# Levels 1 to 3 of a batched triangular inverse on all four quarters of the array, in a two-layer trunk kernel

## What is computed

```python
def chunk_gated_delta_rule(q, k, v, g, beta):
    C = GDN_CHUNK                     # 64
...
    a_mat = jnp.where(strict, jnp.einsum('bhnik,bhnjk->bhnij', k_beta, k) * decay, 0.0) + jnp.eye(C, dtype=f32)
    tri = functools.partial(lax.linalg.triangular_solve, left_side=True, lower=True, unit_diagonal=True)
    u = tri(a_mat, v * beta[..., None])
    w = tri(a_mat, k_beta * jnp.exp(g)[..., None])
...
    S0 = jnp.zeros((B, H, N, v.shape[-1]), f32)
    _, o = lax.scan(step, S0, xs)
```

## Time and profile before

| | |
|---|---|
| time, median of 3 runs | 1431.37 us (1431.27 to 1431.80) |
| the profiled execution's own time | 1431.33 us |
| its span, first to last instruction | 1429.6 us |
| PE busy | 1396.9 us (98%) |
| DVE busy | 668.8 us (47%) |
| ACT busy | 599.9 us (42%) |
| the four tiles' levels 1 to 3 | 11.63, 11.84, 11.85 and 13.17 us |

### The profile page before, as it was taken

How to read it: one execution, slowest core, us unless ns; L and a number is a source line. 1 busy time by engine, 2 the same in 40 slices (tenths; PEclk the granted TensorE clock), 3 DMA queues, 4 the chain that set the end, 5 groups by cost and what they waited for, 6 DMA issues and landing times.

```text
span 1429.6 us, 24988 instructions
## 1 busy us (share of the span) xinstructions
PE 1396.9 (98%) x10495; PEld 1147.7 (80%) x10495; DVE 668.8 (47%) x1112; ACT 599.9 (42%) x866; POOL 526.5 (37%) x239
## 2 busy tenths in 40 slices
PE   7999999999999999999999999999999999999998
PEld 5787778889878888888889977775688888888887
DVE  4665767788753314122144358936543223131231
ACT  5524763445545313232234465568635223131331
POOL 3544332111133543444345224332333443444341
PEclk9999999999999999999999999999999999999999
DMA  5332300000133233223224122210033223323221
GB/s 151 89 101 77 83 20 3 4 4 3 62 104 103 89 96 103 96 88 112 94 89 119 30 89 89 88 60 1 1 102 105 88 88 108 99 88 111 95 89 59
DMA packets 128977, 110.13 MB, mean 77 GB/s; under 512 B 10742, under 2 KB 126576, under 8 KB 128880
## 3 DMA queue, kind: packets, MB, share of 16 engines
q1 hardware_dynamic: 128000, 107.12, 24.1%
q10 hardware_dynamic: 880, 1.59, 0.3%
HBM read 106.60 MB, written 2.10 MB: 76 GB/s over the span
## 4 chain that ended last, share of the span: by engine, by line
PE 91%; DVE 3%; ACT 2%; POOL 2%; issue 1%; DMA 1%; SPq 0%; ACTq 0%; DVEq 0%; POOLq 0%
PE ps L570 23%; PE ps L571 23%; PE ps L575 23%; PE ps L707 5%; PE ps L1141 2%; PE ps L1151 1%; PE ps L1162 1%; PE ps L715 1%; PE ps L607 1%; PE ps L1116 1%; POOL pw_lo L2382 1%; PE ps L938 1%; PE ps L939 1%; PE ps L945 1%; PE ps L722 1%
## 5 line engine op out<-in xcount | busy, mean ns | idle before, releaser
L2469 POOL TENSOR_TENSOR w_lo<-lower,w_hi 128x2048 fp32r<-128x2048 f32 x83 | 385.6, 4645 | 523.6 <-ACT w_hi L1233 508.8
L570 PE MATMUL ps<-h_hi,w_hi 128*128 128x512 f32 x736 | 288.5, 392 | 1.2 <-ACT h_hi L1546 0.8
L571 PE MATMUL ps<-h_hi,w_lo 128*128 128x512 f32 x736 | 286.5, 389 | 0.0
L1233 ACT ACTIVATE w_hi<-lower 128x2048 fp32r<-128x2048 f32 x83 | 158.6, 1910 | 226.2 <-PE ps L575 226.2
L570 PE MATMUL ps<-a_hi,w_hi 128*128 128x512 f32 x480 | 186.7, 389 | 0.0
L571 PE MATMUL ps<-a_hi,w_lo 128*128 128x512 f32 x480 | 186.7, 389 | 0.0
L575 PE MATMUL ps<-h_lo,w_hi 128*128 128x512 f32 x736 | 181.8, 389 | 0.0
L570 PEld LDWEIGHTS ps<-h_hi,w_hi 128*128 128x128 f32 x736 | 138.1, 188 | 33.8 <-issue 4.3
L2174 DVE TENSOR_TENSOR lower<-lower,ps 128x512 f32<-128x512 f32 x60 | 41.3, 688 | 261.3 <-PE ps L575 261.3
L571 PEld LDWEIGHTS ps<-h_hi,w_lo 128*128 128x128 f32 x736 | 138.2, 188 | 29.2 <-issue 0.7
L575 PEld LDWEIGHTS ps<-h_lo,w_hi 128*128 128x128 f32 x736 | 138.1, 188 | 28.8
(11 more groups left out here) (410 smaller groups left out, 2032.0 us busy)
## 6 DMA issues: line engine op xcount, KB each, us to landing
lower<-in_mlp_w_dram SPq DMA_DIRECT2D x64, 1024.0 KB, 5.2
lower<-in_ev_w_in_dram SPq DMA_DIRECT2D x30, 512.0 KB, 3.9
lower<-in_od_w_in_dram SPq DMA_DIRECT2D x10, 1024.0 KB, 5.1
lower<-in_ev_w_out_dram SPq DMA_DIRECT2D x4, 1024.0 KB, 6.2
lower<-in_od_w_out_dram SPq DMA_DIRECT2D x4, 1024.0 KB, 4.9
lower<-in_od_w_in_dram SPq DMA_DIRECT2D x6, 256.0 KB, 3.9
out_dram<-lower SPq DMA_DIRECT2D x6, 256.0 KB, 2.5
upper<-in_x_dram SPq DMA_DIRECT2D x1, 1024.0 KB, 7.2
```

The costliest lines, as they stand in the source:

```text
L570: pe.matmul(o, wh, xh, start=(i_ == 0), stop=False)
L571: pe.matmul(o, wl, xh, start=False, stop=False)
L1233: act.activation(w_high(u)[:, :, 0:w], RAW[:, u % 2, :, 0:w], ACT.Copy).then_inc(hi_ready, 1)
L2469: pool.tensor_tensor(w_low(u)[:, :, 0:w], RAW[:, u % 2, :, 0:w], as_f32(w_high(u)[:, :, 0:w]), ALU.subtract)\
```

## The change

In levels 1 to 3 the products of the odd heads (q = 1) go from row half p to the other column half, and come back in the joined product; the even heads stay. So a group of 16 products uses all four quarters, and it writes two banks, 2g for the even and 2g + 1 for the odd heads. The inverse of an odd head must then lie in the other partition half: PE makes it from TI by a product with the identity EYEC, into bank 4 + g, and ACT copies it to QCR or QCG. DVE transposes only the even heads after levels 0 to 2; after level 3 it transposes both, for level 4, which is as before. Level 0 is as before but for that transpose. New waits are `inv_tr` (ACT for the transposes), `inv_qc` (PE for the copies), and at level 1 one for `r_mkv` and, for s > 0, one for `e_state`.

```diff
+        QCR, QCG = (home("inverse", PAIRS * HD).rearrange("p (j t) -> p j t", j=PAIRS) for _ in range(2))
...
+        def turned_to(s, lev, g):
+            return 2 * (LAST - 2) * s + 2 * (lev - 1) + g + 1
+
+        def crossed_bank(g):
+
+            return ps[:, 2 * g:2 * g + 2, 0:PAIRS * HD].rearrange("p q (j t) -> p j q t", j=PAIRS)
...
+            def crossed_below(s, lev):
+
+                n = 2 * LAST * s + 2 * lev
+                for g, (lt, ti) in enumerate(((LTR, TIR), (LTG, TIG))):
+                    pe.wait_ge(inv_t, n + (2 if lev == 1 else g + 1))
+                    if lev == 1 and g == 1:
+                        pe.wait_ge(r_mkv, s + 1)
+                    for j in range(PAIRS):
+                        for q in range(2):
+                            for p in range(2):
+                                mm = pe.matmul(ps[HALVES[p ^ q], 2 * g + q, j * HD:(j + 1) * HD],
+                                               lt[HALVES[p], j, q, :], ti[HALVES[p], j, q, :], start=True, stop=True)
+                    mm.then_inc(inv_x, 1)
+                    if lev == 1 and s > 0:
+                        pe.wait_ge(e_state, 2 * s + 1)
+                    for j in range(PAIRS):
+                        for p in range(2):
+                            mm = pe.matmul(ps[HALVES[1 - p], 4 + g, j * HD:(j + 1) * HD], ti[HALVES[p], j, 1, :],
+                                           EYEC[HALVES[p], :], start=True, stop=True)
+                    mm.then_inc(inv_tr, 1)
+
+            def crossed_joined(s, lev):
+                n = 2 * LAST * s + 2 * lev
+                for g, (qi, qc, xm) in enumerate(((QIR, QCR, XMR), (QIG, QCG, XMG))):
+                    pe.wait_ge(inv_xm, n + g + 1)
+                    pe.wait_ge(inv_qc, turned_to(s, lev, g))
+                    pe.wait_ge(inv_q, 2 * (LAST - 1) * s + 2 * (lev - 1) + g + 1)
+                    for j in range(PAIRS):
+                        for q in range(2):
+                            for p in range(2):
+                                rows = HALVES[p ^ q]
+                                mm = pe.matmul(ps[HALVES[p], 2 * g + q, j * HD:(j + 1) * HD],
+                                               qc[rows, j, :] if q else qi[s % 2][rows, j, 0, :], xm[rows, j, q, :],
+                                               start=True, stop=True)
+                    mm.then_inc(inv_y, 1)
...
                 for lev in range(1, LAST - 1):
-                    below_blocks(s, lev)
-                    joined_blocks(s, lev)
+                    crossed_below(s, lev)
+                    crossed_joined(s, lev)
...
             def below_blocks(s, lev):
-                for g, xm in enumerate((XMR, XMG)):
+                crossed = 0 < lev < LAST - 1
+                for g, (xm, qc) in enumerate(((XMR, QCR), (XMG, QCG))):
                     act.wait_ge(inv_x, 2 * LAST * s + 2 * lev + g + 1)
-                    act.activation(flat4(xm), bank[g], ACT.Copy, scale=-1.0).then_inc(inv_xm, 1)
+                    act.activation(xm, crossed_bank(g) if crossed else by_head(bank[g]), ACT.Copy, scale=-1.0)\
+                       .then_inc(inv_xm, 1)
+                    if crossed:
+                        act.wait_ge(inv_tr, turned_to(s, lev, g))
+                        act.activation(qc.rearrange("p j t -> p (j t)"), bank[4 + g][:, 0:PAIRS * HD], ACT.Copy)\
+                           .then_inc(inv_qc, 1)
...
-                    dve.copy_predicated(x, blocks(MERGE[:, lev + 1, :]), by_head(bank[g]))\
+                    dve.copy_predicated(x, blocks(MERGE[:, lev + 1, :]),
+                                        crossed_bank(g) if 0 < lev < LAST - 1 else by_head(bank[g]))\
                        .then_inc(inv_t if inner else inv_done, 1)
...
-                        dve.transpose(flat4(qi[s % 2]), flat4(ti)).then_inc(inv_q, 1)
+                        if lev < LAST - 2:
+                            dve.transpose(qi[s % 2][:, :, 0, :], ti[:, :, 0, :]).then_inc(inv_q, 1)
+                        else:
+                            dve.transpose(flat4(qi[s % 2]), flat4(ti)).then_inc(inv_q, 1)
```

More of the change, by code:

```diff
@@ L368, in trunk_kernel @@
              "e_sqg e_sqr e_var e_ln e_rstd e_on r_tr r_tg").split())
-        (inv_m, inv_q0, inv_x, inv_xm, inv_y, inv_t, inv_q, inv_done) = (sem(n) for n in (
-            "inv_m inv_q0 inv_x inv_xm inv_y inv_t inv_q inv_done").split())
+        (inv_m, inv_q0, inv_x, inv_xm, inv_y, inv_t, inv_q, inv_done, inv_tr, inv_qc) = (sem(n) for n in (
+            "inv_m inv_q0 inv_x inv_xm inv_y inv_t inv_q inv_done inv_tr inv_qc").split())
         LAST = LEVELS - 1
```

## The result

| | before | after |
|---|---|---|
| time, median of 7 runs | 1431.37 us (1430.40 to 1432.86) | 1436.46 us (1435.41 to 1436.75) |
| the profiled execution's own time | 1431.33 us | 1435.76 us |
| its span | 1429.6 us | 1434.0 us |
| ratio after to before | | 1.0031, 95% interval 1.0021 to 1.0041 |

The change made the kernel slower by 0.31%, some 4.5 us (4.43 between the two profiled executions, 5.1 between the medians). The forecast was 6.4 us faster. All times in this document were taken at a mean granted clock of 0.994 or more, but for one execution of e_onetr, 1570.44 us at 0.85.

What follows compares the result with a forecast made beforehand. TensorE's issue and the dependent chain of one head group were taken to bind together. Shorter levels gave -1.46, -1.65, -1.66 and -1.65 us for the four tiles, -6.42 in total: 1431.33 - 6.42 = 1424.9 us, range 1422.0 to 1436.5.

Steps and rivals of the forecast that it cites:

- The pace of the array: Products of levels 1 to 3: 58 ns for each quarter with four in use, 0.467 us a group, not 0.935.
- Rivals (2): A matmul pace near 19.5 ns in levels 1 to 3: 1430.3 us, no change to be told; chance 0.14.
- (3): Quarters collide, so a group in levels 1 to 3 still costs 0.935 us: 1440.2 us; chance 0.05.
- The new period: One level of the inverse, start to start: 3.39 us in place of 3.85.
- (a): Below and joined groups of levels 1 to 3 on four quarters: 1.87 us of TensorE less in a level.
- (c): ScalarE's copies of the crossed transposes, 0.38 us each; hidden before the first joined group, with 0.27 us of slack.
- (d): VectorE transposes half as much after levels 0 to 2: 0.28 us less for each of two, mostly slack.
- (e): XM and the merge read two banks with a stride: costs nothing.
- (b): Transposing products added behind each below group: 0.467 us each, 0.93 us of TensorE in a level.
- rival (4): First joined group bound by its copy, the below group using idle quarters: period 3.12 us, 1422.5 us total; chance 0.04.
- Rival (1): Matmul stream itself limited to one pair of weight load and matmul in 27.3 ns: 1438.5 us, slower; chance 0.17.
- (f): New waits at level 1 for s > 0, on r_mkv and e_state: taken at nothing.

Runs made afterwards that it cites:

- e_onetr: The changed kernel with transposing products and copies kept for RWKV alone, left out for GDN: 1432.66 us, ratio to before 1.0004.
- e_banks: The changed kernel, unlooped, with GDN's level 0 in bank 3 instead of bank 1, so the first crossed group waits for RWKV's merge alone: 1436.17 us.
- the two ballasts: The kernel before with the change's transposing products, unread, added once or twice between its own in levels 1 to 3: 1436.56 and 1444.95 us.
- e_notr: The changed kernel with the transposing products and their copies left out for both RWKV and GDN: 1426.95 us, ratio to before 0.9965.

## Why the prediction was wrong

**The pace of the array: right.** The step that I thought most in doubt held. A group of 32 takes 0.69 from its first start to its last end (225.26), and one instruction 0.22, so (0.69 - 0.22)/31 = 15.2 ns an instruction. In the trace's single starts the first four are followed by a gap of 0.09 us, and from then on four start every 58 ns, one in each quarter: 14.6 ns each. Four quarters with 64 columns run together at full pace. Rivals (2) and (3) fall; in particular, two row halves in one bank don't collide. The Trainium skill's rule that different row tiles cannot access the same bank simultaneously (TensorEngine Tiling (Array Packing), "Gotcha 1: PSUM Pressure") isn't what this trace shows, whose two row halves write one bank side by side. The Trainium skill (TensorE: Matmul & The Clock Gate, "Wait — 56ns, not 53.3ns?") has starts never less than about 25 ns apart; the trace differs there too, with 32 instructions in a row some 15 ns apart in four quarters. That the prediction's estimate by that rule, 1436, lies so near the 1436.46 measured is luck.

**The new period: right where nothing breaks it.** 3.41 and 3.50 us for levels 1 and 2 of s = 0, forecast 3.39. XM starts 0.76 after the group's start, QC takes 0.38, VectorE's half transposes 0.42: (a), (c), (d) and (e) hold, and (b) as far as the array goes. One detail came as rival (4) had it: GDN's below group starts in quarters that the transposes leave idle (226.04 against 226.15 for their last start), and the first joined group starts at S + 1.73 in place of 1.92. It shares quarters with the last transposes, though, and its merge comes at S + 2.62, for which the forecast had 2.60.

**Total: wrong, by a term that isn't in the sum.** The step that failed is (b), and with it the new period: I costed the 32 added matmuls of a level at 0.93 us of the array's time and at nothing for the supply of instructions. By the runs they cost up to 27 ns each as a share of a block, 160/127 x 3.4 = 4.28 us a level in place of 3.39. Three such levels are 12.8 us; the stretches are 11.7, 13.6, 13.2 and 12.8, and their mean is 12.8, but s = 0 has only its last level slowed, and s = 1 has the break of 1.62 that the block's pace doesn't explain. Rival (1) came nearest among the priced rivals, with a pace of 27 ns and 1438.5, and had the wrong mechanism: it took the 27 ns of L699 for a limit between two instructions, and I argued it down because each row at 27 to 29 ns could be explained by its quarters. That argument was correct and beside the point. A limit on 256 instructions lets any 100 run at 15 ns, so no short row can exclude it. I gave it 0.17. What would have raised it stood on the page: the packets of instructions, 77 of 16 KB, and the question of how often they come where the matmuls are densest. In this stage of the kernel before they came 3.5 to 4.2 us apart, once 5.2, never nearer.

**(f) New waits: wrong by 1 us.** I named the two waits that are new in name and passed over `2 if lev == 1`, which asks for the second merge. The first product of level 1 for s = 0 starts 1.02 us later than before (225.26 against 224.24). Taking the wait away gave back only 0.3 us by the medians and 0.7 between the merges (e_banks), since the next block is late all the same.

The loss adds up: the spans from first to last merge differ by 4.3 us. The four stretches make 51.3 - 48.5 = 2.8 of it, the later start of level 1 in s = 0 0.9 (1.71 against 0.79 behind the first merge), and of the other 0.64, 0.38 lie between level 4 of s = 2 and level 1 of s = 3 and 0.26 in the last level 4. A block is late there too, at 331.22, but not by that much; this part isn't followed further.

The range reached to 1436.5, and the median, 1436.46, lies just inside its edge; the sign was wrong.

The Trainium skill (Runtime: NRT & Kernel Launch, "Instruction fetch mechanics") says that an engine's instructions are refilled in blocks of 16 KiB, 256 instructions, by the sequencer's own DMA queue, and that this is hidden because instructions issue more slowly than they arrive. The blocks are as the trace shows them (16 KB packets, 127 matmuls with their loads between breaks). That they are hidden is not: at the pace of the groups TensorE would use up 127 matmuls with their loads in 1.9 us (127 x 0.0146), and it gets them in 3.4.

## What to carry to other kernels

Where many small matmuls run in several quarters at once, count TensorE's instructions as a resource of its own: the length of the stage in us against its number of blocks of 256, at the 3.4 us a block measured here. An fp32 product of 64 x 64 is four instructions, so filling idle quarters with extra products is not free, and in a stage already near 29 ns a matmul added instructions can cost more than the array gains: here 16 more a level took the whole gain and 32 more turned it into a loss. Look for "issue" inside a group where no semaphore stands, at equal counts of instructions; where it is found, make fewer instructions, or a loop whose turns are fetched once, and charge the loop its own 0.24 us a turn. And read the clock of the stage itself with a window of its own: a few us at 1.2 GHz don't show in a slice of 36 us.

## What the runs showed of the hardware that I had not expected

- A block of 256 TensorE instructions comes no sooner than 3.2 to 3.5 us after the last: the smallest distance of two instruction packets in this stage was 3.52 us before, 3.31 in the change, 3.29 and 3.22 with the two ballasts. Where TensorE waits in the change, it goes on 2.2 to 2.7 us after a packet's start.
- A loop on TensorE isn't fetched again in turns 2 and 3: 70 packets in place of 80, with 1280 matmuls in the turns 2 and 3 (2560 instructions, ten blocks); in the kernel before 69 in place of 77, with 1024 (2048, eight blocks).
- All four quarters take 64 x 64 fp32 matmuls at 14.6 to 15.2 ns each, 58 to 61 ns in a quarter, against 58 with one quarter alone; two row halves that write one bank at the same time don't slow each other.
- ScalarE copies 64 x 256 fp32 values from one half of the partitions to the other in 0.41 us, GpSimd in 0.40.
- TensorE's granted clock is at 1.2 GHz for a few us in some executions and not in others of the same kernel: from 219.3 to 222.7 us in the profiled one of the change and from 361.7 to 365.1 in that of e_notr; the mean clock of seven executions of the change was 0.998 to 1.000.
